# Three changes to an expert-mixing transformer kernel, joined, and each weight chunk brought by two half transfers

## The reference, cut to what matters

```python
logits = tokens @ router_w                       # 256 x 8
top_vals, top_idx = lax.top_k(logits, 2)
gates = softmax(top_vals)
# for each expert e, over the tokens routed to it:
y = (silu(xb @ w1[e]) * (xb @ w3[e])) @ w2[e]    # 1024 -> 2816 -> 1024
out = out.at[slot_tok].add(y * slot_g)
```

## Time and profile before

| | us |
|---|---|
| median of 3 runs (2025.71 to 2027.35) | 2026.94 |
| the profiled execution | 2017.58 |
| its span, first to last instruction | 2015.8 |
| experts stage from e0's first weight matmul to the end of its matmuls | 784.7 to about 1500 |
| mean granted clock of TensorE, share of full speed | 0.948 |

### The profile page before, as it was taken

One profiled execution on the slowest core, in us unless ns is written; L12 is line 12 of the kernel. 1 busy time (PEld: TensorE's weight loads), 2 busy tenths in 40 slices (PEclk: granted clock), 3 DMA queues, 4 the chain that ended last, 5 costly groups with the idle time before them and its releaser, 6 DMA issues. The chain is left out here.

```text
span 2015.8 us, 43109 instructions
## 1 busy us (share of the span) xinstructions
PE 1842.4 (91%) x18202; PEld 1510.7 (75%) x18202; DVE 826.7 (41%) x2249; ACT 393.1 (20%) x1107; POOL 2.3 (0%) x6
## 2 busy tenths in 40 slices
PE   6999897999989887999999999899979998899987
PEld 4686666888868765789688998698657876688766
DVE  3756552778958812011110111110113676227661
ACT  2232333000014132000000000000012233122331
POOL 0000000000000000000000000000000000000000
PEclk7999998999989887999999999999999999899988
DMA  9622332899973123999999898999993412234100
GB/s 392 238 106 87 123 140 90 312 358 361 378 280 126 42 84 133 420 419 357 373 420 392 315 388 324 421 418 353 363 419 139 167 64 84 84 126 167 43 1 22
DMA packets 67910, 480.22 MB, mean 238 GB/s; under 512 B 7424, under 2 KB 9728, under 8 KB 9856
## 3 DMA queue, kind: packets, MB, share of 16 engines
q1 hardware_dynamic: 67712, 477.39, 60.4%
HBM read 476.31 MB, written 1.05 MB: 237 GB/s over the span
## 5 line engine op out<-in xcount | busy, mean ns | idle before, releaser
L484 PE MATMUL PS<-sb_U,sb_ring 128*128 128x256 f32 (+1 forms) x1456 | 372.6, 413 | 16.3 <-PEq L216 9.9
L484 PEld LDWEIGHTS PS<-sb_U,sb_ring 128*128 128x128 f32 x1456 | 280.7, 196 | 95.6 <-issue 59.4
L1676 PE MATMUL PS<-sb_arena,sb_ring 128*64 128x98 f32 x5632 | 246.3, 247 | 14.3 <-issue 12.2
L1676 PEld LDWEIGHTS PS<-sb_arena,sb_ring 128*64 128x64 f32 x5632 | 240.2, 136 | 21.1 <-issue 18.0
L1704 PE MATMUL PS<-sb_ring,sb_arena 128*64 128x256 f32 x1408 | 161.8, 383 | 5.1 <-issue 4.5
L755 PE MATMUL PS<-sb_U,sb_ring 128*128 128x256 f32 x704 | 155.5, 383 | 4.7 <-PEq L216 4.7
L484 PE MATMUL PS<-sb_arena 128*64 128x128 f32 (+9 forms) x884 | 150.1, 345 | 7.2 <-DVE sb_arena L717 4.4
L755 PEld LDWEIGHTS PS<-sb_U,sb_ring 128*128 128x128 f32 x704 | 134.4, 192 | 25.7 <-issue 7.4
L1704 PEld LDWEIGHTS PS<-sb_ring,sb_arena 128*64 128x64 f32 x1408 | 100.0, 137 | 54.5 <-issue 7.5
L484 PEld LDWEIGHTS PS<-sb_arena 64*128 64x128 f32 (+4 forms) x884 | 106.5, 173 | 45.2 <-issue 24.9
L340 DVE SCALAR_TENSOR_TENSOR sb_arena<-sb_ring,sb_cs,sb_arena 128x256 f32<-128x256 f32 x280 | 135.8, 485 | 10.0
(11 more groups left out here) (343 smaller groups left out, 1615.9 us busy)
## 6 DMA issues: line engine op xcount, KB each, us to landing
sb_ring<-stream SPq DMA_DIRECT2D x450, 1024.0 KB, 7.9
sb_consts<-consts SPq DMA_DIRECT2D x1, 1768.5 KB, 26.6
sb_U<-ctxT SPq DMA_DIRECT2D x1, 1024.0 KB, 6.6
sb_XT<-xT SPq DMA_DIRECT2D x1, 1024.0 KB, 8.4
out<-sb_XT SPq DMA_DIRECT2D x8, 128.0 KB, 2.0
sb_small<-small SPq DMA_DIRECT2D x1, 292.0 KB, 2.9
sb_consts<-consts SPq DMA_DIRECT2D x1, 129.0 KB, 2.8
sb_all_small<-layer_small SPq DMA_DIRECT2D x1, 110.0 KB, 26.8
```

The source lines that it names most:

```text
L484: ins = pe.transpose(o, l, r) if t.turn else pe.matmul(o, l, r, start=s, stop=e)
L1676: ins = pe.matmul(PS[c:c + 64, m % 4, h * T:h * T + n], w[:, h, kt, c:c + 64], src[:, kt, 0:n], start=(kt == 0), stop=(kt == KT - 1))
```

## The change

Four things change together.

**1. Narrower places.** `RANK_CAPS` becomes (98, 88, 80, 72, 64, 64, 64): e3, e4 and e6 work on 88, 80 and 72 columns. The test for `full_flag` now counts, for each distinct size, how many of the seven counts are above it, and compares with how many places are larger (`STEPS`, `LARGER`, a small constant `caps`).

**2. Four homes.** Four chunks of the stream (the chunks 5 to 8 of e0) no longer go to the ring but to four places of their own in the arena (`HOMES`), once. They may be issued as soon as SP is in the stage `pw2`. The other chunks keep going round the ring of 9, so that when the experts stage starts 13 chunks can be on the chip, and after e0 the ring is again all there is.

**3. Freed space.** `UTM` moves from the arena to the half `UC` of `sb_U`, which is free by then, and `GB` moves within the arena, so that the homes fit.

**4. Half transfers.** Each chunk comes by two transfers of 1024 columns (512 KiB) on the same semaphore; the readers wait for 32 in place of 16 per chunk, so for both.

```diff
+PARTS = 2
-RANK_CAPS = (98, 98, 98, 98, 64, 64, 64)
+RANK_CAPS = (98, 88, 80, 72, 64, 64, 64)
+STEPS = sorted(set(RANK_CAPS), reverse=True)
+LARGER = [sum(n > step for n in RANK_CAPS) for step in STEPS]
+HOMES = (6144, 10752, 13104, 15968)
...
+    def home(self, g):
+        return g - self.home_first if self.home_first <= g < self.home_first + len(self.homes) else None
+    def turn(self, g):
+        return g if g < self.home_first else g - len(self.homes)
     def chunk(self, g):
-        return self.ring[:, (g % RING) * CH:(g % RING + 1) * CH]
+        if self.home(g) is not None:
+            return self.homes[self.home(g)]
+        slot = self.turn(g) % RING
+        return self.ring[:, slot * CH:(slot + 1) * CH]
...
     def wait(self, eng, g):
-        eng.wait_ge(self.landed[g % RING], 16 * (g // RING + 1))
+        eng.wait_ge(self.landing(g), 16 * PARTS * (1 if self.home(g) is not None else self.turn(g) // RING + 1))
+    def send(self, sp, g, source):
+        n = CH // PARTS
+        for part in range(PARTS):
+            at = part * n
+            sp.dma_start(self.chunk(g)[:, at:at + n], source[:, at:at + n]).then_inc(self.landing(g), 16)
+    def may_issue(self, g, first, end):
+        if g >= self.total:
+            return False
+        if self.home(g) is not None:
+            return first + RING >= self.home_first
+        return self.before(g) is None or self.before(g) < end
...
-        ws = Stream(nc, ring, a["stream"], landed)
+        ws = Stream(nc, ring, a["stream"], landed, [area(at, CH) for at in HOMES], home_landed, PRE_CH - OUT_CH + RING)
...
-        UTM = area(6144, 2048).rearrange("p (t n) -> p t n", t=2)
+        UTM = UC.rearrange("p k (t c) -> p t k c", t=2)
-        GB = area(10752, T)
+        GB = area(18016, T)
...
-                for g in range(ws.issued, min(last_ch + RING, ws.total)):
-                    old = g - RING - first
-                    if old >= 0:
+                while ws.may_issue(ws.issued, first, last_ch):
+                    g, old = ws.issued, ws.before(ws.issued)
+                    if old is not None and old >= first:
+                        old -= first
...
-                    sp.dma_start(ws.chunk(g), source).then_inc(landed[g % RING], 16)
+                    ws.send(sp, g, source)
+                    ws.issued += 1
```

More of the change, by code:

```diff
@@ L163, with __init__ @@
 class Stream:
-    def __init__(self, nc, ring, dram, sems):
+    def __init__(self, nc, ring, dram, sems, homes, home_sems, home_first):
         self.nc, self.ring, self.dram, self.landed = nc, ring, dram, sems
+        self.homes, self.home_landed, self.home_first = homes, home_sems, home_first
         self.used = self.issued = 0
@@ L183, in load, with before @@
+    def before(self, g):
+        if self.home(g) is not None or self.turn(g) < RING:
+            return None
+        t = self.turn(g) - RING
+        return t if t < self.home_first else t + len(self.homes)
+    def may_issue(self, g, first, end):
[4 more added lines that the diff above has]
+        return self.before(g) is None or self.before(g) < end
     def load(self, sp, first, n, freed):
-        last = min(first + n + RING, self.total)
@@ L187, in load @@
-        for g in range(self.issued, last):
-            old = g - RING
-            if old >= first and old - first < n:
+        while self.may_issue(self.issued, first, first + n):
+            g, old = self.issued, self.before(self.issued)
+            if old is not None and old >= first:
                 sp.wait_ge(*freed[old - first])
-            sp.dma_start(self.chunk(g), self.dram[self.base + g]).then_inc(self.landed[g % RING], 16)
-        self.issued = max(self.issued, last)
+            self.send(sp, g, self.dram[self.base + g])
+            self.issued += 1
@@ L193, in load @@
         self.used = first + n
     def clear(self):
-        clear_together(self.nc, self.landed)
+        clear_together(self.nc, self.landed + self.home_landed)
 class Stage:
@@ L843, in _ @@
                 for g in range(MOD_FIRST):
-                    sp.dma_start(ws.chunk(g), ws.dram[g]).then_inc(landed[g % RING], 16)
+                    ws.send(sp, g, ws.dram[g])
                 sp.dma_start(consts[:, CONST_FIRST:], a["consts"][:, CONST_FIRST:]).then_inc(late, 16)
@@ L1576, in build @@
         rk = area(15152, 560)
-        NR = NE - 1
+        NR, NS = NE - 1, len(STEPS)
         COUNT, KEY, RANK, AT = (rk[:, 8 * i_:8 * i_ + 8] for i_ in range(4))
@@ L1614, in copy_rows @@
                 act.wait_ge(turned, j + 1)
-                nc.scalar.activation(UTM[:, t, 512 * half:512 * half + 512], PS[:, 4 + j, :], ACT.Copy)
+                nc.scalar.activation(UTM[:, t, 4 * half:4 * half + 4, :], PS[:, 4 + j, :].rearrange("p (k c) -> p k c", k=4), ACT.Copy)
         def clear_sum(pool, turned):
```

23 lines of the change are left out of this document (12 added, 11 removed).

## The result

The changed kernel takes 2033.93 us (median of 20 runs, 2019.67 to 2040.07), the kernel before 2025.92 beside it (20 runs): ratio 1.0035, 95% interval 1.0020 to 1.0051. It is slower by 0.35%, where 1981 us were forecast. The profiled execution of the changed kernel is the longest of its 20 (2040.07 us), and that of the kernel before a short one (2017.58), so the 22 us between the two profiles overstate the 8 us between the medians.

What follows compares the result with a forecast made beforehand. PE was taken to bound the 98-column places and weight transfers the 64-column ones. Terms of 5 + 6 + 35 - 0.5 = 46 us off the runs' median 2026.94 gave 1981 us, range 1968 to 2010.

Steps and rivals of the forecast that it cites:

- e1, -6 us: In the second expert place, half transfers shorten the queue code waits behind, so PE's stops vanish: 6 us gained.
- e2 to e7, -35 us: The last six expert places, paced by transfers, take 38 us less than 536.1; 3 left for poor meshing: 35 gained.
- 459 us in all: PE's need in the last six expert places: 3 x 69 + 90.4 + 83.9 + 77.4 us.
- a sign that it is wrong: Transfers that pause in the last six expert places would show the prediction wrong.
- The 44 us of columns: PE time saved in the three narrowed expert places at 0.77 ns per column and pair: 8.2, 14.7 and 21.2 us.
- the first rival's rule: In expert places, each code block takes 6.1 to 6.2 us while transfers are queued, whatever the columns; chance 0.22.
- the 11 us that even the rival gave it: Under the code rival (chance 0.22), the 80-column expert place starts with a full ring and gains 11 of its 14.7 us.
- Halves, 2.50 to 2.56 us a chunk: In weight transfers, splitting 8 KiB rows into two of 4 KiB takes a chunk from 2.50 to 2.56 us.
- The homes, -5 us: 13 chunks instead of 9 are there at e0's start, against PE's idle 5.5 us there: 5 us gained.
- Code stays late: Rival in the experts stage: code delay goes by bytes in flight, not pieces; 20 us gained, 2007 us; chance 0.22.
- Slower: Rival in the last six expert places: each transfer has its own unhidden price, doubled by halving; 2042 us; chance 0.05.
- mostly hidden: Skill's rule on crossing code blocks; by it the second expert place's 6 us could not be won, the sum 40.

Runs made afterwards that it cites:

- e3: Not a run: one of the experts stage's eight places, cut from 98 to 88 columns; 106.7 us in the changed kernel.
- e0: Not a run: the first of the experts stage's eight places; 74.5 us in the kernel before, 71.4 in the changed kernel.
- e1_whole: Changed kernel with whole 1 MiB transfers, narrower places and homes kept; 2010.03 us, ratio 0.9937 to the kernel before.
- e12: As e1_whole, but the seven ranked experts' chunks bring only their first 1024 columns, so results are wrong; 1936.45 us, one run.
- e4_pace2: As e1_whole, but with at most two chunks in the queue throughout the experts stage; 2067.96 us, ratio 1.0200 to the kernel before.
- e17: Changed kernel with each half contiguous in memory, still two transfers of 4 KiB rows; 2020.75 us, ratio 0.9969 to the kernel before.
- e13_homes_only: Kernel before plus the four homes alone, with whole transfers and the old widths; 2020.36 us, ratio 0.9975.
- e16: Changed kernel with each chunk's two transfers taking even and odd partitions, 8 KiB rows; 2010.18 us, ratio 0.9922 to the kernel before.
- e5: Changed kernel with each chunk's two transfers taking 64 neighbouring partitions each, 8 KiB rows; 2549.11 us, ratio 1.2543 to the kernel before.

## Why the prediction was wrong, point by point

**e1, -6 us: the step that failed first.** It said that "with halves the queue behind which a block of code waits is half as long". Counted in transfers it may be, but in bytes and time it isn't, and the wait goes by these: the code starts 3.6 to 3.9 us after the block's start with halves, 3.7 to 3.8 with whole chunks, and e1 went from 104.7 to 105.9.

**e2 to e7, -35 us: the large miss.** The steps that PE then needs 459 us in all, and that the ring is never full again, "so the transfers never pause", rest on the same premise, that no block waits for its code. A place of more than 64 columns has about 17 blocks, and with weights queued each takes about 6.1 us, so it takes 104 to 109 us in the changed kernel and 100 to 104 in the run e1_whole, at 98 columns as at 72. The transfers do pause, at a share of 0.93 in e4, which the prediction named as a sign that it is wrong. From e2 to e7 it is 553 us in place of 501. The 44 us of columns are real (run e12), and less than 10 of them arrive. This was the first rival's rule, and I gave it 0.22 against e4, which ran without a stop. That e4 would stay free of stops was the wrong reading: it gained nothing of the 11 us that even the rival gave it. What let its code through at 98 columns is in part open. A block there lasts 5.4 us, so with 2.4 us from code to start the code can have waited 3.0 at most, an estimate. The engines had no more pauses for it: from 1170 to 1192 us their share is 0.99 at 388 GB/s, as in the run e1_whole's e4 from 1154 to 1180 (0.99, 381), but a chunk landed 5.8 us after its issue and there 7.3. A PE that takes a block in 4.6 us frees chunks sooner and keeps the queue longer; that this is the reason is argued, and the run e4_pace2, with landings of 6.1 us in e4 and stops all the same, doesn't bear it out.

**Halves, 2.50 to 2.56 us a chunk.** Right in size: 2.56. What was missed is the strided reading, 13 to 19 us, which no row of the kernel before could show. Without it the changed kernel would be under the one before by the measured 0.3% (run e17) and still 40 us over the forecast.

**The homes, -5 us.** e0 went from 74.5 to 71.4, and to 70.5 with whole chunks: -3 to -4 (and to 70.0, -4.5, in the run e13_homes_only).

**The rivals.** "Code stays late", 2007 us, had the right mechanism and comes near the run e1_whole, 2010. That is partly luck: of its 20 us the run has 13 to 15, and e4, which was to give 11 of them, gave none; e0, e1, e3 and e6 gave 4, 1, 2 and 4. "Slower" ended on the right side by the wrong mechanism: it set a price per transfer, and there is none (e16). The two rules of the Trainium skill weighed in the prediction: that crossing a block is "mostly hidden" (Runtime: NRT & Kernel Launch, Instruction fetch mechanics) holds in e1 and e3 of the run e12 and in e4 before the change, and fails in the changed kernel, with 59 us of issue (41.2 and 17.9 in the groups above). That each transfer should be 1 MiB or more (DMA: Bandwidth & Descriptors, Rules for kernel authors) is not needed here, where transfers are queued one behind the other: 512 KiB are as fast when the rows are 8 KiB and the partitions even or odd ones (421 GB/s in the run e16).

## What to carry to other kernels

A long weight stream and a long row of small matmuls share the DMA engines: here PE's next block of code waited behind the weights already queued, so look for stops of PE, called "issue", at the same record count each time, before costing an edit that only makes each matmul shorter. Cheaper instructions gained less than 10 of 44 us there; fewer of them should help, which no run here tests. When a transfer is cut, keep its rows long and its source contiguous and let every part touch all groups of partitions: even and odd partitions cost nothing, halves by columns cost 1.0 to 1.4% of the kernel, neighbouring halves by partitions 26%.

## What the runs showed of the hardware

- The next packet of code starts 3.6 to 3.9 us after a block's start in e1, with 8 KiB and with 4 KiB rows, 2.3 to 3.2 with half of the weights (run e12, e6), and 4.4 to 6.3 where a row of 8 KiB takes about 500 ns (run e5, e3). PE goes on some 2.4 us after it (2.5 to 2.9 in the run e5).
- Transfers into 64 neighbouring partitions run at 233 GB/s in place of 420, and into every other partition at 421.
- A short queue is no cheap queue: three halves in flight gave 275 GB/s, two whole chunks 345 to 358, three whole chunks 386 to 397 in e1, e3 and e6, where the run e1_whole had 382 to 388.
- The mean granted clock is 0.97 in e4 and e6 of the changed kernel, where PE stood still for 20 and 22 us, and 1.00 in e1 and e3, where it did for 5 and 13. In e4 and in e6 it was at the lower of its two levels, 1.2 in place of 2.4 GHz, for two stretches of 3.4 us each, so that cost these places some 3 us each, an estimate.
